# The stages behind the delta rule of a two-model kernel: five blocks with barriers made one block with data waits

## The reference

```python
        # qa, ka, va go through a convolution and the gated delta rule (o_a); za, zb, ga, gb are projections
        y_a = rms_norm_2(o_a, dn_norm_w[l]).reshape(b, s, DN_WIDTH) * jax.nn.silu(za)
        y_a = y_a @ w_proj_a[l]                       # 1024 x 1024
        for gi, (win, dil) in enumerate(DIL_CONFIGS): # 3 groups of 4 heads, dilations 1, 4, 16
            o_g, lse_g = dilated_window_attention(qb[:, :, hs], kb[:, :, hs], vb[:, :, hs], win, dil)
        w_g = jax.nn.softmax(jnp.stack(lses, axis=2), axis=2)
        y_b = (o_b * w_g[..., None]).reshape(b, s, ATTN_WIDTH) * jax.nn.silu(zb)
        y_b = y_b @ w_proj_b[l]                       # 768 x 1024
        merged = jax.nn.sigmoid(ga) * y_a + jax.nn.sigmoid(gb) * y_b
        x = x + gate[:, None] * (merged @ w_out[l])
    return rms_norm_2(x, final_norm_w)
```

## Time and profile before

| | |
|---|---|
| median of three runs | 2143.44 us |
| the profiled execution | 2144.82 us, of which its span 2143.1 us |
| PE busy | 2050.6 us (96%) |
| DVE, ACT, POOL busy | 1123.3 (52%), 836.4 (39%), 198.8 us (9%) |
| mean granted clock of TensorE | 0.985 of full speed |
| the part behind the delta rule | from about 1775 us to the end |

### The profile page before, as it was taken

One profiled execution on the slowest core, in us unless ns is written; L12 is line 12 of the kernel. 1 busy time (PEld: TensorE's weight loads), 2 busy tenths in 40 slices (PEclk: granted clock), 3 DMA queues, 4 the chain that ended last, 5 costly groups with the idle time before them and its releaser, 6 DMA issues. The chain is left out here.

```text
span 2143.1 us, 28306 instructions
## 1 busy us (share of the span) xinstructions
PE 2050.6 (96%) x10898; PEld 1683.4 (79%) x10902; DVE 1123.3 (52%) x1971; ACT 836.4 (39%) x1732; POOL 198.8 (9%) x169
## 2 busy tenths in 40 slices
PE   8999999999999999999999999799999998999997
PEld 7777787888887877777888888688787987777776
DVE  5787534423434498734552543589674333225545
ACT  4454633312323344653331332454433335425532
POOL 1331000000000243001000000003031320000100
PEclk9999999999999999999999999999999999999999
DMA  6321022232233332002542433222234223330232
GB/s 185 94 84 41 1 69 86 92 108 85 94 117 90 109 94 79 2 30 80 182 164 97 171 114 109 96 82 89 70 89 136 67 78 106 107 99 30 79 118 79
DMA packets 177527, 198.33 MB, mean 93 GB/s; under 512 B 38755, under 2 KB 140786, under 8 KB 176882
## 3 DMA queue, kind: packets, MB, share of 16 engines
q1 hardware_dynamic: 177394, 196.53, 29.0%
HBM read 180.74 MB, written 11.55 MB: 90 GB/s over the span
## 5 line engine op out<-in xcount | busy, mean ns | idle before, releaser
L161 DVE TENSOR_TENSOR weight_pairs<-weight_ring,weight_pairs 128x1024 fp32r<-128x1024 f32 (+4 forms) x293 | 356.2, 1218 | 439.7 <-ACT weight_pairs L152 439.2
L182 PE MATMUL psum<-operand,weight_pairs 128*128 128x512 f32 x1320 | 527.7, 400 | 18.9 <-PEq L204 13.3
L152 ACT ACTIVATE weight_pairs<-weight_ring 128x1024 fp32r<-128x1024 f32 (+4 forms) x293 | 303.4, 1038 | 566.8 <-PE psum L184 535.2
L183 PE MATMUL psum<-operand,weight_pairs 128*128 128x512 f32 x1320 | 517.7, 392 | 0.0
L184 PE MATMUL psum<-operand,weight_pairs 128*128 128x512 f32 x1320 | 517.5, 392 | 0.0
L182 PEld LDWEIGHTS psum<-operand,weight_pairs 128*128 128x128 f32 x1320 | 249.6, 189 | 80.3 <-issue 23.1
L184 PEld LDWEIGHTS psum<-operand,weight_pairs 128*128 128x128 f32 x1320 | 249.2, 189 | 53.8
L183 PEld LDWEIGHTS psum<-operand,weight_pairs 128*128 128x128 f32 x1320 | 249.8, 189 | 50.8 <-issue 1.0
L182 PE MATMUL psum<-weight_pairs,hidden 128*128 128x512 f32 x512 | 200.1, 391 | 0.0
L184 PE MATMUL psum<-weight_pairs,hidden 128*128 128x512 f32 x512 | 199.3, 389 | 0.0
L183 PE MATMUL psum<-weight_pairs,hidden 128*128 128x512 f32 x512 | 199.2, 389 | 0.0
(11 more groups left out here) (419 smaller groups left out, 2774.7 us busy)
## 6 DMA issues: line engine op xcount, KB each, us to landing
weight_ring<-in_w_in_dram SPq DMA_DIRECT2D x100, 512.0 KB, 3.5
weight_ring<-in_w_up_dram SPq DMA_DIRECT2D x64, 512.0 KB, 3.6
weight_ring<-in_w_down_dram SPq DMA_DIRECT2D x64, 512.0 KB, 3.5
weight_ring<-in_w_out_dram SPq DMA_DIRECT2D x24, 512.0 KB, 3.5
ada_rows<-in_ada_w_dram SPq DMA_DIRECT2D x24, 512.0 KB, 4.6
spilled<-v_t SPq DMA_DIRECT2D x22, 256.0 KB, 4.1
weight_ring<-in_w_in_dram SPq DMA_DIRECT2D x20, 256.0 KB, 2.9
weight_ring<-in_w_proj_a_dram SPq DMA_DIRECT2D x8, 512.0 KB, 3.9
```

The lines of the kernel that those rows point to most:

```text
L152: act.activation(self.pairs[:, i % SPLIT_RING, 0, 0:n], self.buf[:, i % RING, 0:n], ACT.Copy).then_inc(self.rounded, 1)
L161: dve.tensor_tensor(self.pairs[:, i % SPLIT_RING, 1, 0:n], self.buf[:, i % RING, 0:n], self.pairs[:, i % SPLIT_RING, 0, 0:n].bitcast(F32), ...
L182: pe.matmul(out, lhs[0], rhs[0], start=start, stop=False)
L183: pe.matmul(out, lhs[0], rhs[1], start=False, stop=False)
```

## The change

The five stages share one block. A `Part` holds the semaphores of all of them and one `clear` comes at the end of the last; the order of each engine's programs is unchanged, and where a barrier stood, the engines wait for what they need:

- PE waits, before the row gate product, for all low halves of `y_pair` and, before each pair of output chunks, for the last readers of its banks. The banks of this product are rotated: chunks 0 to 7 go to banks 4, 5, 6, 7, 0, 1, 2, 3. DVE waits for the sigmoid of chunk c before its multiplication.
- PE waits before the scores for q, k and v, before the scores of pair 0 for six and before those of pair 1 for eight multiplications.
- The 30 matmuls at the end of this attention are gone (`idle` is 0 here, 30 elsewhere).
- SP waits for all scores before it sends for zb; PE waits for all exponentials before the first gate item.
- In the last stage PE waits for each low half before the first chunk that reads it, and for the banks; SP sends one weight item, waits for the low halves, and then reloads x; it waits for the products with silu(zb) before it loads the last gain.
- In `PROJECT_ORDER` the piece with the eight sigmoids comes three "dense" later.

Most of the diff is a change of indentation. Cut to what differs:

```diff
+class Part:
+    def __init__(self, nc, ctx):
+        self.nc, self.ctx, self.block, self.made = nc, ctx, None, []
+    def sems(self, prefix, names):
+        made = [self.ctx.enter_context(self.nc.semaphore(f"{prefix}_{n}")) for n in names.split()]
+        self.made += made
+        return made
+
+@contextmanager
+def part(nc):
+    with ExitStack() as ctx:
+        p = Part(nc, ctx)
+        with nc.Block() as block:
+            p.block = block
+            yield p
+        clear(nc, p.made)
...
-def attention(nc, psum, jobs, stores, ident, ident_half, probs, probs_t, o_rows, stats, sems, besides=None):
+def attention(block, psum, jobs, stores, ident, ident_half, probs, probs_t, o_rows, stats, sems, besides=None, ready=(),
+              freed=None, idle=30):
...
+            if freed is not None and p < len(freed[1]):
+                pe.wait_ge(freed[0], freed[1][p])
...
+        for sem, count_needed in ready:
+            pe.wait_ge(sem, count_needed)
...
-            keep_busy(pe, psum[:, 0, :], ident_half, 30)
+        keep_busy(pe, psum[:, 0, :], ident_half, idle)
...
-def product_by_channels(pe, psum, banks, weights, pair, chunks):
+def product_by_channels(pe, psum, banks, weights, pair, chunks, written=None):
...
+                if written is not None and h == 0:
+                    pe.wait_ge(written, k + kk + 1)
...
-def channel_products(nc, psum, weights, pair, chunks, epilogues, loads=None):
+def row_gate_products(part, psum, weights, pair, pair_ready, merged, gate_ready, bank_free):
...
+    @block.tensor
+    def _(pe):
+        pe.wait_ge(*pair_ready)
+        for c in range(0, KD, 2):
+            pe.wait_ge(*bank_free[c // 2])
+            product_by_channels(pe, psum, ((c + 4) % 8, (c + 5) % 8), weights, pair, KD)
...
+    @block.vector
+    def _(dve):
+        for c in range(KD):
+            weights.low(dve, start + c + 1)
+            dve.wait_ge(weights.items_done, start + 2 * (c // 2) + 2)
+            dve.wait_ge(gate_ready, c + 1)
+            dve.tensor_tensor(merged[:, c, :], psum[:, (c + 4) % 8, :], merged[:, c, :], ALU.mult).then_inc(times_done, 1)
...
+            with part(nc) as merge:
+                stored, v_stored, low, gate_ready = projected_and_gated(
...
+                times_done = row_gate_products(merge, psum, weights, y_pair, (low, H), merged, gate_ready,
+                                               ((v_stored, KB), (v_stored, KB), (stored, 3 * KB), (stored, 3 * KB)))
+                scores_done, powers_done = dilated_attention(
+                    merge, ((stored, 3 * KB), (v_stored, KB)), (times_done, (KD - 2, KD)), psum, q, k, v, y, stats, KB,
+                    window_incl_half, causal_half, residues_half, ident, ident_half, sb)
...
 PROJECT_ORDER = ("dense dense gated dense gated dense gated dense gated dense gated dense gated dense gated dense gated dense gated "
-                 "dense gated dense dense gated dense dense dense dense dense dense").split()
+                 "dense gated dense dense dense dense dense gated dense dense dense").split()
...
-            sp.wait_ge(z_landed, 16)
-            sp.wait_ge(gate_landed, 16)
...
     @block.sync
     def _(sp):
+        sp.wait_ge(*scores_done)
         sp.dma_start(z, spilled_z.rearrange("c p s -> p c s")).then_inc(z_landed, 16)
         weights.send(sp, base + KD)
         sp.wait_ge(z_landed, 16)
...
+                if p == 0:
+                    pe.wait_ge(*powers_done)
...
     @block.sync
     def _(sp):
+        weights.send(sp, start + 1)
+        sp.wait_ge(y_low, C)
         sp.dma_start(x[:], x_kept[:]).then_inc(x_landed, 16)
         weights.send(sp, last)
+        sp.wait_ge(z_weighted, C)
         tail.load_gain(sp, gain_row)
...
         for c in range(0, KD, 2):
+            if c < 4:
+                pe.wait_ge(gate_stored, 6 + c)
+            else:
+                pe.wait_ge(banks_weighed, C)
-            product_by_channels(pe, psum, (c, c + 1), weights, y_pair, C)
+            product_by_channels(pe, psum, (c, c + 1), weights, y_pair, C, y_low if c == 0 else None)
```

More of the change, by code:

```diff
@@ L650, in at_run @@
         return (p - lag) // 4 if p >= lag and (p - lag) % 4 == 0 and (p - lag) // 4 < runs else None
[L652 to L656, removed]
-                for j in pair:
[L658 to L689, removed]
@@ L690, in values @@
                     if split_copies and j % 2:
-                        pe.wait_ge(copied_dve, p + 1)
+                        pe.wait_ge(copied_dve, p)
                     elif split_copies:
-                        pe.wait_ge(copied_act, p + 1)
+                        pe.wait_ge(copied_act, p)
                     else:
[L695 to L718, removed]
@@ L719, in _ @@
-            keep_busy(pe, psum[:, 0, :], ident_half, 30)
[L721 to L734, removed]
-                else:
[L736 to L801, removed]
-                if at_run(p, SINKS) in with_sinks:
-                    shift_sinks(at_run(p, SINKS))
-                if split_copies and 0 <= p - TURN < pairs:
-                    copy(p - TURN)
-                if at_run(p, FINISH) is not None:
-                    finish(at_run(p, FINISH))
-                if in_pairs and at_run(p, STORE) is not None:
-                    store_low(at_run(p, STORE))
@@ new lines, in flip @@
+        def flip(run):
+            pe.wait_ge(normed, run + 1)
+            for t in range(T):
+                mm = pe.transpose(psum[:, OUT + run % 2, t * P:(t + 1) * P], o_rows[:, run % 2, t * P:(t + 1) * P],
+                                  ident[:])
+            mm.then_inc(flipped, 1)
+        for sem, count_needed in ready:
+            pe.wait_ge(sem, count_needed)
+        for p in range(pairs + STORE + 1):
+            if p < pairs:
+                scores(p)
+            if 0 <= p - VALUES < pairs:
+                values(p - VALUES)
+            if 0 <= p - TURN < pairs:
+                turn(p - TURN)
+            if at_run(p, FLIP) is not None:
+                flip(at_run(p, FLIP))
@@ L2604, in same, with _ @@
-def same(bank):
-    return bank
+    end = start + KD
+    times_done, = part.sems("rows", "times_done")
+    block = part.block
+    @block.sync
+    def _(sp):
+        weights.send(sp, end)
+    @block.tensor
+    def _(pe):
+        pe.wait_ge(*pair_ready)
+        for c in range(0, KD, 2):
+            pe.wait_ge(*bank_free[c // 2])
+            product_by_channels(pe, psum, ((c + 4) % 8, (c + 5) % 8), weights, pair, KD)
+    @block.scalar
+    def _(act):
+        for c in range(KD):
+            weights.high(act, start + c + 1)
@@ L2890, in dilated_attention @@
+    return stored, v_stored, low, gate_ready
+def dilated_attention(part, ready, freed, psum, q, k, v, y, stats, C, window_incl, causal, residues, ident, ident_half, sb):
     jobs = []
@@ new lines, in merged_and_last_products, with _ @@
+    sems = part.sems("last", TAIL_SEMS + " x_landed gate_taken merged_done high low out_landed")
+    block = part.block
+    x_landed, gate_taken, merged_done, high, low, out_landed = sems[-6:]
+    tail = Residual(psum, x, weights, ident, eps, small, work, None, sems[:-6])
+    @block.sync
+    def _(sp):
+        weights.send(sp, start + 1)
+        sp.wait_ge(y_low, C)
+        sp.dma_start(x[:], x_kept[:]).then_inc(x_landed, 16)
+        weights.send(sp, last)
+        sp.wait_ge(z_weighted, C)
+        tail.load_gain(sp, gain_row)
+        weights.send(sp, last + 2 * per_half)
+        for t in range(T):
+            sp.wait_ge(tail.scaled, t + 1)
+            sp.dma_start(out[0, t * P:(t + 1) * P, :], tail.rows[:, t % T, :]).then_inc(out_landed, 16)
+        sp.wait_ge(out_landed, 16 * T)
```

872 lines of the change are left out of this document (467 added, 405 removed).

## The result

Median of eleven runs 2120.44 us (2118.01 to 2133.07), beside 2143.42 of the kernel before in as many; ratio 0.991 with a 95% interval of 0.9889 to 0.993, that is 15 to 24 us less. Forecast were 2122.4 us and 21.0 less; the medians differ by 23.0. The profiled execution took 2118.66, its span 2116.9.

The account below looks back on a forecast made before the run. PE is busy 96% of the span, so only its standing or lower-clock time can be won. 6.84 + 4.53 + 2.1 + 3.40 + 4.13 = 21.0 us off 2144.82 gives 2123.8; the median lies 1.4 lower: 2122.4, range 2118 to 2128.5.

Parts of the forecast that it names:

- Sigmoids: Projection: sigmoids three items later remove a 4.55 us PE stall and 2.29 us of clock, gain 6.84 us; cover 1.6 us.
- rival 1: Sigmoids stall PE at the new place, 4.5 us of the gain gone: 2126.9 us; chance 0.08.
- Barrier before the row gate product: Between projection and row gate product: 2.82 us of standing and 1.71 of clock, gain 4.53 us.
- Barrier before the attention: Before the dilated attention's scores: pair 1 starts 1.7 us earlier; gain 2.1 us, between 1.7 and 3.9.
- Barrier and fillers before the gates: Last transposes to first gate product: barrier and 30 fillers gone, gain 3.40 us, clock expected to stay 1.00.
- rival 2: Clock falls all the same, at the attention and, without fillers, at the gates: 2 us less gain, 2124.4; chance 0.12.
- In the gates: Gate stage: the waits inside, at the lower clock, hang on PE's own second item and move along; gain 0.
- Barrier before the last stage: Between gates and last stage: 2.45 us of standing and 1.68 of clock, gain 4.13 us.
- rival 3: Barriers only covered something else holding PE as long, so only the sigmoids' 6.84 us remain: 2136.6; chance 0.04.
- rival 4: Slower: without fillers the clock stays at 1.2 GHz from attention into the gate product, 38.4 us: 2160.8; chance 0.03.
- The upper end: Whole kernel: 2128.5 us, from rivals 1 and 2 with 1.5 us of scatter.

Follow-up runs that it names:

- run 1: Kernel before with only the sigmoids three items later, all barriers kept: 2136.08 us against 2140.98, ratio 0.9971.
- run 2: Changed kernel with the sigmoids back at their old place, no barriers: 2132.11 us, ratio 0.9955.
- run 7: Changed kernel with 36 filling matmuls on PE between the scores of pair 0 and pair 1: 2120.91 us.
- run 10: Run 8 with 26 filling matmuls behind the scores of pair 1: 2119.27 us, ratio 0.9891.
- run 11: Changed kernel with PE waiting for the last gate sigmoids before the last stage, a stop of 1.3 us: 2125.25 us, one execution.
- run 12: Changed kernel with PE waiting for the third weight item's split before the last stage, a stop of 3.1 us: 2135.53 us, one execution.
- run 3: Changed kernel with SP sending for the zb rows only after the attention's last output is stored: 2127.6 us.
- run 4: Changed kernel with the 30 filling matmuls at the attention's end again: 2124.9 us.
- run 6: Changed kernel with DVE leaving the last weight subtraction of the row gate part to the gate stage: 2119.27 us.
- run 8: Changed kernel with row gate banks 4, 5, 0, 1, 2, 3, 6, 7 and the last weight subtraction left to the gate stage: 2120.61 us.
- run 5: Changed kernel with the row gate product in banks 0 to 7 in order, waits adapted: 2120.42 us.

## Why the prediction was right, point by point

- **Sigmoids**: 6.93 for 6.84, and run 1 shows it alone (6.4), run 2 in reverse (7.0). Cover 1.8 for 1.6; rival 1 did not come.
- **Barrier before the row gate product**: 4.54 for 4.53, standing and clock both as read from the trace.
- **Barrier before the attention**: the step that failed. "I take 2.1", with ends 1.7 and 3.9, was 0.63. Pair 1 did start 1.7 us earlier. I then took the ramp for a chain of latencies that moves as a whole. It did not: the lead was 2.0 us at the third pair and 0.6 when the clock was back, because the low clock ended 1.1 us later behind the last product than before and lay on matmuls for its whole length. I had the fall ("the clock may fall as before") and took its price for unchanged; run 7, with the wait filled, shows that 2.3 us of this attention were the clock's.
- **Barrier and fillers before the gates**: 3.49 for 3.40. Without the fillers the clock stayed up in the changed kernel's profile, as forecast. But the reason, that waits shorter than 1.56 us leave it up, does not hold: behind the same 1.02 us wait it was low in runs 2, 10, 11 and 12, four of the eleven traces without fillers. So this half of rival 2 holds in part of the executions, at 1.5 to 1.7 us.
- **In the gates**: "the waits inside move along" was wrong by 3.87 us. About 2.3 us of it came with DVE's maximum no longer beside POOL's products (run 3): PE's stop of 0.68 went, and with it half of the 6.8 us at the low clock behind the first spread. That much is left in runs 4, 6, 7 and 8, which have no stop at the spread and take 54.0 us from the first to the last gate product; this is a comparison of traces, no run changes the stop alone. The other 1.6 us are luck of the execution: in the profiled runs of the changed kernel and in run 5 the clock did not fall at the first spread at all; in eight traces (runs 2, 4, 6, 7, 8, 10, 11, 12) it fell there with no stop before it. What decides this I did not find.
- **Barrier before the last stage**: 4.18 for 4.13.
- **End**: 0.99 us more from the last product to the end, in every kernel with the one block (11.2, against 10.2 in run 1 and before). DVE's last instruction starts 4.6 us behind the last product in both; the difference lies in the last `clear`. `clear` makes one barrier for each group of neighbouring semaphore numbers, and the semaphores of the one block fall into five groups where those of the last stage alone fell into three. One round takes 0.4 to 0.5 us. The clears at the end of the program, before and after (times, ns shortest/median/longest, first and last start):

```profile
L204 POOLq EVENT_SEMAPHORE_RANGE_CLEAR  x3: 46/66/92, 2142.1 to 2142.9; - x3
L230 POOLq EVENT_SEMAPHORE_RANGE_CLEAR  x5: 44/110/154, 2114.8 to 2116.7; - x5
```


The single stops were priced right, to 0.1 us each, in four of the five terms. That the sum came out within 1.7 us is luck all the same: the misses at the attention (-1.5) and at the end (-1.0) stand against 3.9 in the gates, and none of the three was forecast. Of the rivals, 3 and 4 found nothing in the trace. The upper end, 2128.5, would have been passed by three of the eleven runs (2131.41 to 2133.07, mean clock 0.983 to 0.984, against 0.988 to 0.991). No trace of these three was taken; runs 2 and 12, at 0.984 and 0.983, make it likely that they are executions in which the attention ran at the low clock for 20 us. I didn't find what decides it.

## What to carry to other kernels

A stage barrier costs PE its standing time and, here at stops from 2.5 us on, between half as much and as much again at the lower clock (1.7 us behind 2.5 and 2.8, 3.0 behind 3.1); both can be read from starts of matmuls before the change. When it is replaced by a data wait, price the clock behind that wait too, above all where the matmuls that follow are small. Read what the barrier kept apart: here a transfer released early took POOL's work out of DVE's way, worth about 2.3 us by the comparison of traces above. Read whether a stretch has the same falls of the clock in more than one trace before counting on it. And look at the numbers of a block's semaphores: its end costs a barrier round for each group of neighbouring ones (making it one group was not tried).

## What the runs showed of the hardware

- **DVE beside POOL.** A maximum of two SBUF operands of 4x512 took 0.68 us alone and 1.64 or 1.66 while POOL's 128x512 products ran; copies from PSUM (2.10 us for three) took the same beside POOL's products as when these ended halfway. The Trainium skill ("GPSIMD Engine Reference", section "1. Specifications") says that POOL shares its SBUF interfaces with VectorE and contends with instructions that have two SBUF inputs: the trace agrees, with 0.96 us more for this one instruction. It is not the same for all: a weight subtraction, also with two SBUF inputs, took 1.30 us beside the products and 1.23 alone.
- **The table load.** 1.28 us, and the sigmoid started 1.29 after its start, the copies ahead of it having just ended. The 1.38 us of drain that the Trainium skill ("ScalarE: Activation LUTs", section "What ACT_TABLE_LOAD costs") adds did not show.
- **The clock has a long low state under small matmuls.** Behind the same 2.43 us stop the attention's matmuls (64 to 256 columns) ran at 1.2 GHz for 6.7 us in five traces and for about 20 in two (0.52 and 0.53 over 20.3 and 19.4 us), with PE counted as busy throughout. Behind stops before products of 512 columns it was 3.5 to 7 us in every trace.
- **Stops and the clock.** Behind 1.2, 1.3 and 1.56 us of standing before dense work it was 1.00; behind 2.3 to 4.4 us it was 0.50. In the attention it was 0.50 behind 1.82 us (run 8) and behind 0.74 and 1.01 us with a short burst between (run 6), and behind one wait of 1.02 us in four traces of eleven.
- **A fall without a stop.** Behind the second spread, six matmuls with 4 partitions of input among dense products, the clock was at 0.50 for 3.4 us in every trace but that of run 3, with PE busy throughout; behind the first spread in eight of the eleven in which no stop lay there.
- **Barriers in `clear`.** One round of the barrier with its range clear took 0.4 to 0.5 us; the number of rounds follows the gaps in the semaphore numbers (three before, five in the one block).
